# Residual rows of five tiles: turned by TensorE into PSUM, or read back from DRAM in lanes and turned by VectorE in 32x32 squares

## What is computed

```
x   = x + W_out [ pool_mixer(u) ; stickbreak_attn(q, k, v) ]     # u, q, k, v from RMSNorm(x) W_in
n   = RMSNorm(x) * norm_ffn
g   = argmax(softmax(n @ w_group))                               # 4 groups
top = top_k((n @ w_expert)[group g], 2)                          # 8 experts a group, 32 in all
y   = x + sum over the 2 experts of gate * (silu(n @ w_gate[e]) * (n @ w_up[e])) @ w_down[e]
```

## Time and profile before

| what | value |
|---|---|
| time, median of 3 runs | 1083.18 us (1082.81 to 1083.39) |
| the profiled execution's own time | 1083.24 us |
| its span in the trace | 1081.5 us |
| PE busy | 1038.1 us, 96% of the span |
| DVE busy | 541.1 us, 50% |
| ACT busy | 305.9 us, 28% |
| POOL busy | 173.4 us, 16% |
| read and written in DRAM | 272.98 MB and 42.87 MB |
| mean granted TensorE clock | 0.99 |

### The profile page before, as it was taken

One profiled execution on the slowest core, in us unless ns is written; L12 is line 12 of the kernel. 1 busy time (PEld: TensorE's weight loads), 2 busy tenths in 40 slices (PEclk: granted clock), 3 DMA queues, 4 the chain that ended last, 5 costly groups with the idle time before them and its releaser, 6 DMA issues.

```text
span 1081.5 us, 29154 instructions
## 1 busy us (share of the span) xinstructions
PE 1038.1 (96%) x12741; PEld 820.4 (76%) x12741; DVE 541.1 (50%) x1060; ACT 305.9 (28%) x588; POOL 173.4 (16%) x155
## 2 busy tenths in 40 slices
PE   8999999999999989999999999999999889898896
PEld 7999999977666559999867898656897556465665
DVE  5326664558875544345644455455544434343431
ACT  6323332356775552223311101110111010101011
POOL 0001200599300000100101111111111111111102
PEclk9999999999999999999899999999999999999999
DMA  7357785000126469675999999999999999999993
GB/s 249 112 163 212 219 274 157 1 14 3 39 76 199 123 229 302 224 270 208 353 383 399 380 387 373 391 380 383 371 388 384 381 388 389 390 388 383 390 387 101
DMA packets 85816, 293.19 MB, mean 271 GB/s; under 512 B 13425, under 2 KB 44849, under 8 KB 60069
## 3 DMA queue, kind: packets, MB, share of 16 engines
q1 hardware_dynamic: 78277, 273.30, 67.9%
q0 software_dynamic: 7280, 17.58, 6.9%
q10 hardware_dynamic: 128, 0.39, 0.1%
HBM read 272.98 MB, written 42.87 MB: 292 GB/s over the span
## 4 chain that ended last, share of the span: by engine, by line
PE 74%; DMA 17%; SPq 5%; DVE 2%; ACT 1%; issue 1%; POOL 0%; ACTq 0%; POOLq 0%
PE bank L2874 20%; DMA w_all<-in_w_up 15%; PE bank L2417 12%; PE bank L2653 8%; SPq L1059 5%; PE bank L2460 4%; PE bank L2891 4%; PE bank L2588 3%; PE bank L2895 3%; PE bank L2625 3%; PE bank L2498 3%; PE bank L2899 2%; PE bank L2520 1%; PE bank L2740 1%; DMA pgv<-v_scr 1%; PE bank L2413 1%
## 5 line engine op out<-in xcount | busy, mean ns | idle before, releaser
L2874 PE MATMUL bank<-w_all,xeT 128*32 128x256 f32 x6144 | 346.9, 383 | 22.0 <-DMA w_all<-in_w_up 19.1
L2874 PEld LDWEIGHTS bank<-w_all,xeT 128*32 128x32 f32 x6144 | 253.0, 111 | 110.0 <-issue 30.3
L2244 DVE STREAM_TRANSPOSE xeT<-xg 32x256 f32<-32x256 f32 x360 | 156.4, 434 | 89.5 <-DMA xg<-n_scr,tab 84.4
L2891 PE MATMUL bank<-w_all,hT 128*32 128x256 f32 x744 | 165.6, 379 | 0.0
L2895 PE MATMUL bank<-w_all,hT 128*32 128x512 f32 x744 | 129.3, 592 | 0.0
L1928 DVE TENSOR_TENSOR_SCAN keep<-keep,unseen 128x1024 f32<-128x1024 f32 (+7 forms) x64 | 95.8, 1528 | 33.9 <-ACT keep L1451 33.9
L2417 PE MATMUL bank<-w_hi,xh 128*128 128x256 f32 x376 | 108.1, 288 | 0.1
L2417 PE MATMUL bank<-w_hi,xl 128*128 128x256 f32 x376 | 105.5, 281 | 0.0
L2417 PE MATMUL bank<-w_lo,xh 128*128 128x256 f32 x376 | 105.5, 280 | 0.0
L2891 PEld LDWEIGHTS bank<-w_all,hT 128*32 128x32 f32 x744 | 81.8, 110 | 29.8
L1699 ACT ACTIVATE sgl<-bank 128x384 f32<-128x384 f32 x32 | 15.7, 491 | 305.6 <-PE bank L2874 305.6
(11 more groups left out here) (316 smaller groups left out, 1483.5 us busy)
## 6 DMA issues: line engine op xcount, KB each, us to landing
w_all<-in_w_down SPq DMA_DIRECT2D x64, 1024.0 KB, 31.1
w_all<-in_w_gate SPq DMA_DIRECT2D x64, 1024.0 KB, 30.9
w_all<-in_w_up SPq DMA_DIRECT2D x64, 1024.0 KB, 31.8
k_scr<-in_cache_k SPq DMA_DIRECT2D x32, 256.0 KB, 3.1
v_scr<-in_cache_v SPq DMA_DIRECT2D x32, 256.0 KB, 3.5
pgk<-k_scr SPq DMA_DIRECT2D x32, 256.0 KB, 4.0
w_raw<-in_w_in SPq DMA_DIRECT2D x7, 1024.0 KB, 6.8
pgv<-v_scr SPq DMA_DIRECT2D x4, 1024.0 KB, 6.4
```

The source lines that it names most:

```text
L2244: last = dve.transpose(xeT[i][rows_of(s), :, rows_of(g)], lane[:, :, s, :])
L2874: lasts = [pe.matmul(pair_ps(i)[rows_of(q), g, :, :], xeT[i][:, k, rows_of(g)], pair_of(b, i, k, q), start=(k == 0 and g != 1), stop=(k == ...
L2891: return pe.matmul(y_right_ps(g), hT[:, ft, rows_of(g)], w[ft // 2][:, ft % 2, DA:D], start=first and g != 1, stop=ends, skip_group_check= ...
```

## The change

For tiles 0 to 4 (`LANED = 5`) the transposes on TensorE and the copies by ScalarE go. In their place ScalarE waits for the tile's row store to `y_all` and reads the tile back with four DMAs. Transfer l takes feature columns 256 l to 256 l + 255 of all 128 rows and puts them on the 32 partitions 32 l to 32 l + 31 of one buffer, `lanes_in`: partition 32 l + r holds the rows r, 32 + r, 64 + r and 96 + r, 256 columns each. VectorE turns the buffer in 32x32 squares into `nT` with one instruction (`turn_lanes`). The partitions of `nT` then hold other features than before: partition 32 l + j, chunk k is feature 256 l + 32 k + j. GpSimd therefore copies the router weights, after the gain, into a second buffer `w_l` of that order in 16 pieces.

The logits of tile t-2 (t = 2 to 6) now stand behind (1, t), not those of tile t-1 behind (2, t). Their scaling on VectorE stands behind the add of (1, t), and `mark(0)` and `shift(0)` behind the add and scaling of (1, 4). Tiles 5 to 8 are turned as before; their semaphore is `s_xT`, used for another purpose earlier in the kernel.

New waits: SP's store of tile t (t = 1 to 5) for the lanes of tile t-1; ScalarE's reading back for the row store and, as there is one lane buffer, for the turn of the tile before; VectorE's turn for the lanes. SP's two loads at t = 3 no longer wait for transposes.

```diff
+    LANED = 5
+    SIDE = P // 4
+    LCOLS = D // 4
+    LANE_DMAS = 16 * 4
+    lanes_in, _ = place("lanes_in", [P, P // SIDE, LCOLS], F32, at_late)
+    w_l, at = place("w_l", [P, KT, NGRP + NE], F32, at_b)
...
-    at_tmp = at_late + 4 * 2 * NB * (CAP + 2 * NE)
+    at_tmp = at_late + 4 * D
...
             def store_residual(t):
                 r = ROWS[t]
                 sp.wait_ge(s_xm, tile_done(t))
+                if 1 <= t <= LANED:
+                    sp.wait_ge(s_lane, LANE_DMAS * t)
                 sp.dma_start(y_all[row0(t):row0(t) + r, :], xmid[0:r, t, :]).then_inc(s_yst, 16)
...
                     sp.wait_ge(s_yst, 16 * (t + 1))
-                    sp.wait_ge(s_n2T, t + 1)
+                    if t == 7:
+                        sp.wait_ge(s_xT, NT + t + 1 - LANED)
                     if t == 3:
                         load_part(2)
...
-            pool.tensor_tensor(w_r[:, :, :], w_r[:, :, :], gain, ALU.mult).then_inc(s_wg, 1)
+            chain.link(pool.tensor_tensor(w_r[:, :, :], w_r[:, :, :], gain, ALU.mult))
+            for l in range(4):
+                for s in range(4):
+                    move = pool.tensor_copy(w_l[SIDE * l:SIDE * l + SIDE, :, :].rearrange("p (y s) e -> p y s e", s=4)[:, :, s, :],
+                                            w_r[SIDE * s:SIDE * s + SIDE, 2 * l:2 * l + 2, :])
+                    if (l, s) != (3, 3):
+                        chain.link(move)
+            move.then_inc(s_wg, 1)
+            pool.wait_ge(s_wg, 1)
...
+            def rows_to_lanes(t):
+                act.wait_ge(s_yst, 16 * (t + 1))
+                if t >= 1:
+                    act.wait_ge(s_n2c, t)
+                rows = y_all[row0(t):row0(t) + P, :].rearrange("(g r) (l c) -> l r g c", r=SIDE, c=LCOLS)
+                for l in range(4):
+                    act.dma_start(lanes_in[SIDE * l:SIDE * l + SIDE, :, :], rows[l]).then_inc(s_lane, 16)
...
             for t in range(LAST):
-                if t >= 1:
+                if t > LANED:
                     copy_turned(t - 1)
                 square_mid(t)
                 root_mid(t)
+                if t < LANED:
+                    rows_to_lanes(t)
...
+            def turn_lanes(t):
+
+                dve.wait_ge(s_lane, LANE_DMAS * (t + 1))
+                if t >= 2:
+                    dve.wait_ge(s_lgp, t - 1)
+                dve.transpose(nT[t % 2][:, :, :].rearrange("p k (g r) -> p g k r", r=SIDE), lanes_in[:, :, :]).then_inc(s_n2c, 1)
...
                 dve.tensor_tensor(dst, out_ps(s)[0:r, :], dst, ALU.add).then_inc(s_xm, 1)
+                if n == 1 and 2 <= t < LANED + 2:
+                    scale_logits(t - 2)
+                if n == 1 and t == 4:
+                    mark(0)
+                    shift(0)
                 if n == NO - 1:
...
                     norm_scale(t)
-                    if 1 <= t < LAST:
+                    if 1 <= t <= LANED:
+                        turn_lanes(t - 1)
+                    if LANED < t < LAST:
                         scale_logits(t - 1)
-                    if t in (3, 6):
-                        mark(t // 3 - 1)
-                        shift(t // 3 - 1)
+                    if t == 6:
+                        mark(1)
+                        shift(1)
...
-                    last = pe.matmul(logit_ps(t)[0:r, :], nT[t % 2][:, k, 0:r], w_r[:, k, :],
+                    last = pe.matmul(logit_ps(t)[0:r, :], nT[t % 2][:, k, 0:r], (w_l if t < LANED else w_r)[:, k, :],
                                      start=(k == 0), stop=(k == KT - 1))
...
                 n, t = wsteps[s]
-                if n == 1 and t >= 1:
+                if n == 1 and 2 <= t < LANED + 2:
+                    logits(t - 2)
+                if n == 1 and t > LANED:
                     transpose_mid(t - 1)
                 if n == NO - 1 and t >= 1:
-                    logits(t - 1)
+                    if t > LANED:
+                        logits(t - 1)
```

More of the change, by code:

```diff
@@ L297, in hybrid_step @@
     assert at <= at_t
+    LANED = 5
[4 more added lines that the diff above has]
+    w_l, at = place("w_l", [P, KT, NGRP + NE], F32, at_b)
+    assert at <= at_t
     gffn, at = place("gffn", [P, D], F32, at_u)
@@ L522, in hybrid_step @@
     s_xs = sem("x_normed")
-    s_xT = sem("x_transposed")
+    s_xT = sem("x_transposed_then_last_residual_rows_transposed")
     s_xh = sem("x_hi_ready")
@@ L590, in hybrid_step @@
     s_n2 = sem("ffn_normed")
-    s_n2T = sem("ffn_transposed")
+    s_lane = sem("residual_rows_in_lanes")
     s_n2c = sem("ffn_copied")
@@ L1633, in copy_turned @@
                 r = ROWS[i]
-                act.wait_ge(s_n2T, i + 1)
-                if i >= 2:
-                    act.wait_ge(s_lgp, i - 1)
+                act.wait_ge(s_xT, NT + i + 1 - LANED)
+                act.wait_ge(s_lgp, i - 1)
                 act.activation(nT[i % 2][:, :, 0:r], norm_ps(i)[:, :, 0:r], ACT.Copy).then_inc(s_n2c, 1)
+            def rows_to_lanes(t):
[5 more added lines that the diff above has]
+                    act.dma_start(lanes_in[SIDE * l:SIDE * l + SIDE, :, :], rows[l]).then_inc(s_lane, 16)
             def square_mid(t):
@@ L2143, in turn_copied @@
                 r, k = ROWS[LAST], TURNS[part]
-                dve.wait_ge(s_n2T, NT + part)
+                dve.wait_ge(s_xT, NT + NT - LANED + part)
                 dve.wait_ge(s_lgp, LAST - 1)
                 dve.tensor_copy(nT[LAST % 2][:, k, 0:r], last_norm_ps(part)[:, :, 0:r]).then_inc(s_n2c, 1)
+            def turn_lanes(t):
[3 more added lines that the diff above has]
+                dve.transpose(nT[t % 2][:, :, :].rearrange("p k (g r) -> p g k r", r=SIDE), lanes_in[:, :, :]).then_inc(s_n2c, 1)
             def scale_logits(t):
@@ L2746, in transpose_mid @@
                 pe.wait_ge(s_xm, tile_done(t) - (1 if KT - 1 not in ks else 0))
-                if t >= 1 and ks[0] == 0:
+                if ks[0] == 0:
                     pe.wait_ge(s_n2c, t)
@@ L2751, in transpose_mid @@
                     last = pe.transpose(out, xmid[0:r, t, k * P:(k + 1) * P], ident[0:r, 0:r])
-                last.then_inc(s_n2T, 1)
+                last.then_inc(s_xT, 1)
             def ranks(q):
```

## The result

The changed kernel takes 1088.10 us (median of 10, 1084.45 to 1091.94), the kernel before 1082.51 us beside it (median of 10, 1081.02 to 1084.42). The ratio is 1.0049, 95% interval 1.0035 to 1.0062: slower by half a per cent. The median lies 0.7 us above the upper end of the predicted range.

The account below looks back on a forecast made before the run. The prediction took the end to be set by a weight stream full from about 514 us, started by the TensorE-bound stage before; -4.25 + 0.6 + 1.4 + 2.3 + 0 = +0.05 us gave 1083.3 us, range 1080.9 to 1087.4.

Parts of the forecast that it names:

- Removed work: On TensorE, five of nine tiles lose their transposes: 0.85 us saved a tile, -4.25 us in all (-3.95 to -4.5).
- The turn: On VectorE, one 128x1024 instruction takes 1.30 us (1.15 to 1.54); logits 1 and 2 wait 0.3 us each, +0.6.
- Logits 0: TensorE waits for tile 0's lanes, landed 5.5 us after first issue, and their turn: +1.4 us (0.3 to 3.9).
- The marking: On VectorE, the first marking, moved between tile 4's adds, makes logits 3 wait: +2.3 us (2.0 to 2.7).
- "Nothing more" for the later lanes: Loop of store, lanes and next store takes 8.7 us against a tile of 10.4, so later lanes cost nothing.
- These have over 3 us of room because of the marking: Tile 3's lanes, beside `load_part(2)` coming about 3 us earlier, have over 3 us to spare, so no cost.
- rival B: Lanes land late, 8 us after first issue, so logits 0 to 3 wait: +4.2 us, 1087.4 us; chance 0.22.
- A wait costed at its own length: Each TensorE wait ahead of logits 0 to 3 entered the sum as its duration: 0.6, 1.4 and 2.3 us.
- The bytes: DMA reads 2.6 MB more at 444 to 490 us, covered by idle engine time: 0, without cover 6.7 us.
- rival E: Slower: lane reads push weight loads past 514 us, +6.7 us, 1090.0 us; chance 0.05.
- Rival D: Slower: a tile's four lane transfers run one after another, 11.6 us a tile, 1105.3 us; chance 0.05.
- Passing on to the end: If the stage from 435 to 514 us ends X us earlier, the weight stream and the end come X earlier.

Follow-up runs that it names:

- the second profile: The changed kernel run once more, unaltered, for another profile: 1088.46 us, ratio 1.0052, profiled at 1090.31 us.
- the last experiment: Changed kernel with four tiles in lanes, turn and logits half a tile later, stores not waiting for lanes, `load_part(2)` held, marking moved: 1079.86 us, 0.9992 of the kernel before.
- the kernel with the hold: Changed kernel with the first marking behind tile 3's turn and `load_part(2)` held until tile 3's lanes have landed: 1090.38 us, ratio 1.0067 to the kernel before.
- the kernel with the hold and the earlier first store: Changed kernel with the marking moved, `load_part(2)` held for tile 3's lanes, and tile 0's store and rows ahead of its loads: 1090.23 us, ratio 1.0078.

## Why the prediction was wrong

Two steps failed above all. The sum prices each wait of TensorE at its own length and puts the clock behind it at nothing; the clock cost 4.5 us more in the profiled execution. And it puts the meeting of `load_part(2)` with tile 3's lanes at nothing; in the second profile it was worth a gap of 4.36 us. Term by term:

*Removed work: right in kind, 0.70 us a tile against 0.85.* A tile without a wait at the low clock takes 10.33 us instead of 11.03. Part of the rest is the short wait for the turn at logits 1 and 2, predicted at 0.3 each. In the last experiment, where nothing waits, it is 10.15, 0.88 less.

*The turn: right.* 1.22 us against 1.30.

*Logits 0: near in size, for another reason.* Predicted 1.4, measured 2.11 and 1.15 in the two profiles. The lanes landed at about 445.8 + 3.5 = 449.3, the 449.25 of the estimate. What failed in this term is the price of the issues: 0.56 us each (2.25 for four), not 0.38, on an engine that owes VectorE a square. That made tile 1's scaling, behind which the turn stands, 2 us late, not 0.8.

*The marking: right, but not alone.* The add of tile 4 came some 2 us late and logits 3 waited 1.82, predicted 2.3.

*"Nothing more" for the later lanes: the loop was too short in the sum.* It was put at 8.7 us for store and lanes, against a tile of 10.4. The changed kernel's stores of tiles 1 to 3 on SP (start, us of the issue):

```profile
449.38 0.34 SPq L1097 DMA_DIRECT2D out_y_all<-xmid  x1
...
459.84 0.34 SPq L1097 DMA_DIRECT2D out_y_all<-xmid  x1
...
470.42 0.34 SPq L1097 DMA_DIRECT2D out_y_all<-xmid  x1
```

A round is 10.5 us, as long as a quiet tile (10.33), and had no room; in the second round ScalarE also waits some 1.9 us for the turn of the one lane buffer. In the kernel with the hold the chain that ended last runs through this loop alone from the first lanes to tile 4's, with stores at 448.28, 458.70, 469.75 and 480.86. This fits that a wait mended at one tile came back at another.

*"These have over 3 us of room because of the marking": wrong.* The prediction saw that `load_part(2)` comes earlier, next to tile 3's lanes, and cost that at nothing. The slowest of tile 3's lanes took 9.4 to 11.8 us from its own issue to landing there (changed kernel and the three runs that leave those loads as they were), not 5.5 from the first issue. With the marking out of the way the wait became 5.39 us instead of vanishing. That is rival B's mechanism, late lanes, at one tile. That it sets the median is likely, as the second profile, above the median, has it, but two profiles do not show it. The Trainium skill, "DMA: Bandwidth & Descriptors", section "Issuing engines are not separate DMA queues", says that transfers from different issuing engines run on the same DMA engines and interleave; the traces agree: a lane took 2.4 to 3.1 us with SP quiet, 7.0 to 11.8 beside two of its 1 MB loads.

*A wait costed at its own length: wrong, the largest step.* Each wait on TensorE went into the sum as so many us. Two of them were followed by some 7 and 3 us at 1.2 GHz; in the profiled execution that cost 4.5 us, without which the stage would have come out 0.4 us longer, not 4.9, and the kernel of before with one gap of 2.29 us shows it by itself. Product 2 of tile 6, forecast to end near 500 us, has its add at 505.02. With this term alone the sum of +0.05 becomes +4.55, 1087.8 us (an estimate). That this comes near the median is partly luck, as the lanes of tile 3 came later still in the second profile; and that the first profiled execution, 1084.56 us, falls inside the range is luck too, by its clock behind the stage.

*The bytes: right as far as seen.* 508 to 514 us is now full, but 514 to 520 us stands at 0.35: the idle stretch has moved with the stage, not gone. So rival E's sign came true for another reason; no run prices the bytes by themselves. Rival D, 11.6 us for four lanes one after another, is not what happened: four lanes of 2.4 to 3.0 us each, issued some 0.5 us apart, were all in within 4.6 us. The Trainium skill, "SBUF — State Buffer", section "Can I just issue two DMAs to hit both halves?", says that two such transfers serialize; the rival's reading of it, whole durations in a row, is what the traces contradict, and whether the data moved one after another within the 4.6 us no run here shows.

*Passing on to the end: about right.* The gap of 2.29 us delayed the stage by 4.0 and the kernel by 2.7 (1.3 to 4.1 by the interval). The second profile's stage ends 6.1 us later than before, and its time is 7.1 us longer. A gain passed on less well: 3.6 us became 2.1 at most.

## What to carry to other kernels

A tight schedule on TensorE is not priced by the sum of its waits alone: look behind each gap for the granted clock, and count those microseconds as well. When work is taken off a full engine and sent on a round through other queues, compare the length of the round with the time between two results, and give it slack instead of hurrying it: none of the attempts to speed up the round here removed the waits, while half a tile more, together with stores that no longer waited for lanes and one tile less, did. And ask of each wait that a change drops, like SP's for the transposes, what it kept apart.

## What the runs showed that was not expected

- A short gap is followed by half the clock in some cases and not in others. Gaps of 1.21 and 1.01 us passed at 1.00; gaps of 0.74, 0.86 and 1.15 us were followed by 0.5 to 0.6; all of 1.8 us and more were. Even the 0.52 us ahead of logits 2, in the kernel with the hold and the earlier first store, was followed by 0.52 at 475 to 478 us. The length of the gap alone does not decide; what else does is open.
- A store of 512 KB behind a 1 MB load of the same queue took 7.5 us to landing, and 9.0 behind two (2.9 to 3.0 with the queue clear, in the changed kernel). The order on SP's queue moved a landing by 4.5 to 6 us.
- An issue on ScalarE of a lane transfer takes a median of 0.45 us with no load of SP beside it and up to 1.3 beside the large loads, and all of it lies ahead of the next square.
